# Column weights of an expert norm: folded into the expert weights, or put on the transposed rows

## The reference, cut to what matters

```python
h = h + concat(ssd_out, gmlp_out) @ w_out
h = h + hierarchical_moe(rms_norm(h, norm_ffn), ...)
h = h + sigmoid(rms_norm(h, norm_pg) @ w_pg) * rms_norm(p @ w_ple, norm_ple)

def rms_norm(x, g):
    return x * rsqrt(mean(x * x) + EPS) * g

def hierarchical_moe(t, ...):          # two experts of each row, weights comb
    for e in range(16):
        hid = silu(t @ w_gate[e]) * (t @ w_up[e])      # 1024 -> 512, twice
        y = y + comb[:, e:e + 1] * (hid @ w_down[e])   # 512 -> 1024
```

## Time and profile before

| what | value |
|---|---|
| time, median of 3 runs | 1126.4 us (1124.49 to 1126.66) |
| time of the profiled execution | 1126.14 us |
| its span on the core | 1124.2 us |
| TensorE busy | 1055.3 us (94%) |
| VectorE busy | 701.7 us (62%) |
| ScalarE busy | 504.2 us (45%) |
| POOL busy | 196.7 us (17%) |
| STT pieces of gate and up, line 1524 | 264, mean 747 ns |
| ACTIVATE pieces of gate and up, line 1920 | 264, mean 712 ns |

### The profile page before, as it was taken

One profiled execution on the slowest core, in us unless ns is written; L12 is line 12 of the kernel. 1 busy time (PEld: TensorE's weight loads), 2 busy tenths in 40 slices (PEclk: granted clock), 3 DMA queues, 4 the chain that ended last, 5 costly groups with the idle time before them and its releaser, 6 DMA issues.

```text
span 1124.2 us, 17530 instructions
## 1 busy us (share of the span) xinstructions
PE 1055.3 (94%) x6221; PEld 910.3 (81%) x6222; DVE 701.7 (62%) x1099; ACT 504.2 (45%) x872; POOL 196.7 (17%) x348
## 2 busy tenths in 40 slices
PE   7999999998999999946999999999999999999896
PEld 5777799985776788746988999898899999878685
DVE  4422575824867667256599566999946753576664
ACT  6733312033111122151588457787845652564332
POOL 3611000102233112111001000101000000065542
PEclk9999999999999999856999999999999999999998
DMA  8893400221513362157499675999966644142541
GB/s 333 269 273 73 171 1 1 76 79 56 179 61 87 109 247 85 57 179 261 140 371 372 241 278 206 384 353 384 358 237 256 239 178 168 57 168 82 166 146 56
DMA packets 71703, 209.01 MB, mean 186 GB/s; under 512 B 10863, under 2 KB 36079, under 8 KB 58730
## 3 DMA queue, kind: packets, MB, share of 16 engines
q1 hardware_dynamic: 61546, 174.02, 43.5%
q0 software_dynamic: 6512, 21.77, 5.5%
q10 hardware_dynamic: 3600, 12.62, 2.8%
HBM read 169.74 MB, written 38.65 MB: 185 GB/s over the span
## 4 chain that ended last, share of the span: by engine, by line
PE 57%; DVE 10%; issue 5%; ACT 3%; DVEq 1%; DMA 0%; POOL 0%; POOLq 0%; ACTq 0%; another core or an unknown queue 0%
PE bank L605 13%; PE bank L607 12%; PE bank L606 12%; PE bank L599 4%; DVE w_lo L1524 4%; PE bank L850 3%; PE bank L852 3%; PE bank L851 3%; PE bank L593 2%; ACT w_hi L1920 2%; PE bank L821 1%; PE bank L788 1%; DVE w_lo L1051 1%; PE bank L807 1%; PE bank L814 1%
## 5 line engine op out<-in xcount | busy, mean ns | idle before, releaser
L605 PE MATMUL bank<-w_hi,xh 128*128 128x256 f32 x768 | 220.7, 287 | 2.7 <-DVE xl L1051 2.7
L606 PE MATMUL bank<-w_lo,xh 128*128 128x256 f32 x768 | 218.4, 284 | 0.0
L607 PE MATMUL bank<-w_hi,xl 128*128 128x256 f32 x768 | 218.4, 284 | 0.0
L1524 DVE SCALAR_TENSOR_TENSOR w_lo<-raw_gu,cols,w_hi 128x512 fp32r<-128x512 f32 x264 | 178.0, 747 | 7.4 <-ACT w_hi L1920 6.3
L1920 ACT ACTIVATE w_hi<-raw_gu,cols 128x512 fp32r<-128x512 f32 x264 | 165.4, 712 | 21.1 <-PE bank L607 16.4
L605 PEld LDWEIGHTS bank<-w_hi,xh 128*128 128x128 f32 x768 | 147.9, 193 | 5.4 <-issue 3.1
L606 PEld LDWEIGHTS bank<-w_lo,xh 128*128 128x128 f32 x768 | 148.1, 193 | 0.5
L607 PEld LDWEIGHTS bank<-w_hi,xl 128*128 128x128 f32 x768 | 148.0, 193 | 0.0
L605 PE MATMUL bank<-w_hi,hid_hi 128*128 128x512 f32 x192 | 80.6, 420 | 11.6 <-DVE hid_lo L1051 11.6
L2230 POOL COPY index_u<-token_u 128x1 uint32 (+1 forms) x25 | 7.8, 311 | 428.2 <-PE bank L599 405.4
L607 PE MATMUL bank<-w_hi,hid_lo 128*128 128x512 f32 x192 | 75.3, 392 | 0.0
(11 more groups left out here) (373 smaller groups left out, 2195.6 us busy)
## 6 DMA issues: line engine op xcount, KB each, us to landing
raw_gu<-in_w_gate_up SPq DMA_DIRECT2D x64, 1024.0 KB, 4.9
raw_d<-in_w_down_rows SPq DMA_DIRECT2D x32, 1024.0 KB, 6.7
y_rows<-yb ACTq DMA_DIRECT2D x24, 512.0 KB, 6.4
raw_w<-in_w_in_blocks SPq DMA_DIRECT2D x20, 512.0 KB, 6.5
y_rows<-ones SPq DMA_DIRECT2D x16, 512.0 KB, 6.5
xr<-in_x_prompt_t SPq DMA_DIRECT2D x8, 512.0 KB, 9.2
xst<-in_x_prompt SPq DMA_DIRECT2D x8, 512.0 KB, 10.0
raw_o<-in_w_out SPq DMA_DIRECT2D x8, 512.0 KB, 3.6
```

The costliest lines, as they stand in the source:

```text
L605: nc.tensor.matmul(out, lh(k), rh(k), start=(k == 0), stop=False)
L606: nc.tensor.matmul(out, lh(k), rl(k), start=False, stop=False)
L607: last = nc.tensor.matmul(out, ll(k), rh(k), start=False, stop=(k == (K or len(ks)) - 1))
L1524: ins = V.scalar_tensor_tensor(out=gu_lo[:, k, :, cols_], in0=raw_gu[q // KC][:, k, :, :], scalar=gain(e, k), in1=gu_hi[:, k, :, cols_].bi ...
```

## The change

The expert weights are split as they are, without the columns `g`. A piece of gate and up is now two rows of 128 at once, 128x1024, a plain copy on ScalarE and a plain subtraction on VectorE, and counts two steps. The columns `g` go on the transposed rows instead: `b_xT` takes them from the banks in eight pieces of 128x128, each with its column as scale (ScalarE) or as the scalar of an STT (VectorE). Only the last of the eight counts in `xh_ready` or `xT_ready`; behind it stands a wait for the other seven. The projection of the gate stage keeps its pieces of 128x512 with columns, in functions of their own (`pg_low`, `pg_high`).

```diff
 # VectorE, split(e, at)
+                if isinstance(e, int) and e == NE:
+                    for q in steps:
+                        dve.wait_ge(s("w_high"), done + q + 1)
+                        pg_low(q // KC, q % KC)
+                elif steps[0] < 2 * KC:
+                    for q in steps[::2]:
+                        dve.wait_ge(s("w_high"), done + q + 2)
                         k, cols_ = q % KC, slice(q // KC * HE, (q // KC + 1) * HE)
-                        ins = V.scalar_tensor_tensor(out=gu_lo[:, k, :, cols_], in0=raw_gu[q // KC][:, k, :, :], scalar=gain(e, k),
-                                                     in1=gu_hi[:, k, :, cols_].bitcast(F32), op0=ALU.mult, op1=ALU.subtract)
+                        lo(gu_lo[:, k:k + 2, :, cols_], raw_gu[q // KC][:, k:k + 2, :, :], gu_hi[:, k:k + 2, :, cols_]).then_inc(s("w_split"), 2)
...
+            def pg_low(half, k):
+                cols_ = slice(half * HE, (half + 1) * HE)
+                V.scalar_tensor_tensor(out=gu_lo[:, k, :, cols_], in0=raw_gu[half][:, k, :, :], scalar=gain(NE, k),
+                                       in1=gu_hi[:, k, :, cols_].bitcast(F32), op0=ALU.mult, op1=ALU.subtract).then_inc(s("w_split"), 1)
...
             def b_xT(n):
                 dve.wait_ge(s("xh_ready"), n)
-                own.did(lo(xl[:, 0:4].rearrange("p k t -> p (k t)"), bank[0][:, :], xh[:, 0:4].rearrange("p k t -> p (k t)")))
-                lo(xl[:, 4:8].rearrange("p k t -> p (k t)"), bank[1][:, :], xh[:, 4:8].rearrange("p k t -> p (k t)")).then_inc(s("xT_ready"), 1)
+                for k in range(KC):
+                    ins = V.scalar_tensor_tensor(out=xl[:, k, :], in0=bank[k // 4][:, k % 4 * P:(k % 4 + 1) * P], scalar=gain(0, k),
+                                                 in1=xh[:, k, :].bitcast(F32), op0=ALU.mult, op1=ALU.subtract)
+                    if k + 1 < KC:
+                        own.did(ins)
+                    else:
+                        own.wait()
+                        ins.then_inc(s("xT_ready"), 1)
...
 # ScalarE, split(e, at)
+                    elif x2 and e == NE:
+                        pg_high(q // KC, q % KC)
+                    elif q % 2 == 0:
                         k, cols_ = q % KC, slice(q // KC * HE, (q // KC + 1) * HE)
-                        ins = A.activation(gu_hi[:, k, :, cols_], raw_gu[q // KC][:, k, :, :], ACT.Copy, scale=gain(e, k))
+                        A.activation(gu_hi[:, k:k + 2, :, cols_], raw_gu[q // KC][:, k:k + 2, :, :], ACT.Copy).then_inc(s("w_high"), 2)
...
             def b_xT(n):
                 act.wait_ge(s("xTp_done"), n)
-                own.did(A.activation(xh[:, 0:4].rearrange("p k t -> p (k t)"), bank[0][:, :], ACT.Copy))
-                own.wait()
-                A.activation(xh[:, 4:8].rearrange("p k t -> p (k t)"), bank[1][:, :], ACT.Copy).then_inc(s("xh_ready"), 1)
+                for k in range(KC):
+                    ins = A.activation(xh[:, k, :], bank[k // 4][:, k % 4 * P:(k % 4 + 1) * P], ACT.Copy, scale=gain(0, k))
+                    if k + 1 < KC:
+                        own.did(ins)
+                    else:
+                        own.wait()
+                        ins.then_inc(s("xh_ready"), 1)
```

More of the change, by code:

```diff
@@ L1519, in split @@
                 steps = SPLITS[at]
-                for q in steps:
-                    dve.wait_ge(s("w_high"), done + q + 1)
-                    if q < 2 * KC:
+                if isinstance(e, int) and e == NE:
[5 more added lines that the diff above has]
+                        dve.wait_ge(s("w_high"), done + q + 2)
                         k, cols_ = q % KC, slice(q // KC * HE, (q // KC + 1) * HE)
-                        ins = V.scalar_tensor_tensor(out=gu_lo[:, k, :, cols_], in0=raw_gu[q // KC][:, k, :, :], scalar=gain(e, k),
-                                                     in1=gu_hi[:, k, :, cols_].bitcast(F32), op0=ALU.mult, op1=ALU.subtract)
-                    else:
+                        lo(gu_lo[:, k:k + 2, :, cols_], raw_gu[q // KC][:, k:k + 2, :, :], gu_hi[:, k:k + 2, :, cols_]).then_inc(s("w_split"), 2)
+                else:
+                    for q in steps:
+                        dve.wait_ge(s("w_high"), done + q + 1)
                         ks = q - 2 * KC
-                        ins = lo(d_lo[:, ks, :], raw_d[:, ks, :], d_hi[:, ks, :])
-                    ins.then_inc(s("w_split"), 1)
+                        lo(d_lo[:, ks, :], raw_d[:, ks, :], d_hi[:, ks, :]).then_inc(s("w_split"), 1)
+            def pg_low(half, k):
+                cols_ = slice(half * HE, (half + 1) * HE)
+                V.scalar_tensor_tensor(out=gu_lo[:, k, :, cols_], in0=raw_gu[half][:, k, :, :], scalar=gain(NE, k),
+                                       in1=gu_hi[:, k, :, cols_].bitcast(F32), op0=ALU.mult, op1=ALU.subtract).then_inc(s("w_split"), 1)
             def final_ple(k):
@@ L1536, in final_pg @@
                 dve.wait_ge(s("w_high"), STEPS * NE + KC + PC + k + 1)
-                cols_ = slice(half * HE, (half + 1) * HE)
-                V.scalar_tensor_tensor(out=gu_lo[:, k, :, cols_], in0=raw_gu[half][:, k, :, :], scalar=gain(NE, k),
-                                       in1=gu_hi[:, k, :, cols_].bitcast(F32), op0=ALU.mult, op1=ALU.subtract).then_inc(s("w_split"), 1)
+                pg_low(half, k)
             def b_xT(n):
                 dve.wait_ge(s("xh_ready"), n)
-                own.did(lo(xl[:, 0:4].rearrange("p k t -> p (k t)"), bank[0][:, :], xh[:, 0:4].rearrange("p k t -> p (k t)")))
-                lo(xl[:, 4:8].rearrange("p k t -> p (k t)"), bank[1][:, :], xh[:, 4:8].rearrange("p k t -> p (k t)")).then_inc(s("xT_ready"), 1)
+                for k in range(KC):
[6 more added lines that the diff above has]
+                        ins.then_inc(s("xT_ready"), 1)
             def b_hidT(half, ready):
@@ L1917, in split, with pg_high @@
                         act.wait_ge(s(name), 16 * (e + earlier + 1) if x2 else act.snap(16 * e + 16 * earlier + 16))
-                    if q < 2 * KC:
-                        k, cols_ = q % KC, slice(q // KC * HE, (q // KC + 1) * HE)
-                        ins = A.activation(gu_hi[:, k, :, cols_], raw_gu[q // KC][:, k, :, :], ACT.Copy, scale=gain(e, k))
[L1921 to L1924, removed]
+                    if q >= 2 * KC:
+                        ks = q - 2 * KC
+                        A.activation(d_hi[:, ks, :], raw_d[:, ks, :], ACT.Copy).then_inc(s("w_high"), 1)
+                    elif x2 and e == NE:
+                        pg_high(q // KC, q % KC)
+                    elif q % 2 == 0:
+                        k, cols_ = q % KC, slice(q // KC * HE, (q // KC + 1) * HE)
+                        A.activation(gu_hi[:, k:k + 2, :, cols_], raw_gu[q // KC][:, k:k + 2, :, :], ACT.Copy).then_inc(s("w_high"), 2)
+            def pg_high(half, k):
+                cols_ = slice(half * HE, (half + 1) * HE)
+                A.activation(gu_hi[:, k, :, cols_], raw_gu[half][:, k, :, :], ACT.Copy, scale=gain(NE, k)).then_inc(s("w_high"), 1)
             def b_xT(n):
                 act.wait_ge(s("xTp_done"), n)
-                own.did(A.activation(xh[:, 0:4].rearrange("p k t -> p (k t)"), bank[0][:, :], ACT.Copy))
-                own.wait()
-                A.activation(xh[:, 4:8].rearrange("p k t -> p (k t)"), bank[1][:, :], ACT.Copy).then_inc(s("xh_ready"), 1)
+                for k in range(KC):
+                    ins = A.activation(xh[:, k, :], bank[k // 4][:, k % 4 * P:(k % 4 + 1) * P], ACT.Copy, scale=gain(0, k))
+                    if k + 1 < KC:
+                        own.did(ins)
+                    else:
+                        own.wait()
+                        ins.then_inc(s("xh_ready"), 1)
             def b_hidT(half, ready):
@@ L1948, in final_pg @@
                     act.wait_ge(s(f"w{2 * half + 2 * k // KC}_loaded"), 16 * (NE + 8))
-                cols_ = slice(half * HE, (half + 1) * HE)
-                A.activation(gu_hi[:, k, :, cols_], raw_gu[half][:, k, :, :], ACT.Copy, scale=gain(NE, k)).then_inc(s("w_high"), 1)
+                pg_high(half, k)
             def one_block(b, e, splits, more):
```

## The result

The changed kernel takes 1161.7 us (median of 4 runs, 1161.12 to 1162.28) against 1126.5 for the kernel before on the same chip (4 runs): ratio 1.0314, interval 1.0292 to 1.0335, slower by 35 us. The profiled execution has a span of 1160.5 us, 36.3 more than before.

A forecast was written before the change was run, and what follows sets the result against it. TensorE, busy 94%, was taken to bound the kernel, with `xh`, `xl`, `hid_lo` in series setting its expert-stage waits. 25 g - 11.7, with g = 1.88, gave +35 us on 1126.14: 1161 us, range 1138 to 1177.

The forecast's parts named there:

- The chain `xh`, `xl`, `hid_lo`: Expert stage, from the transposes' end to the down product's third quarter: 2.9 us without slack, additions move TensorE one for one.
- `xh` +1.00: ScalarE in `b_xT`: eight pieces with a column take 2.23 us against 1.23 before, +1.00 us.
- `xl` +0.88: VectorE in `b_xT`: eight pieces until the next start take 2.08 us against 1.20 before, +0.88 us.
- g = 1.88: Growth of the serial row-split work per block in `b_xT`, 1.00 + 0.88 us; bounds 0.7 to 3.2.
- Periods 20.47, 23 of them 470.8 us: Between down-product starts: short periods 18.59 + 1.88 = 20.47 us, long ones the same; all 23 together +31.6 us.
- First block +1.9: First `b_xT` stands in the open before the first matmul, where TensorE waits 2.7 us for `xl`: +1.9 us.
- The end +1.9: After the last block the gate stage waits for VectorE's projection-weight split, queued behind the last `xl`: about +1.9 us.
- the long periods: Nine down-product periods of 19.85 us: the wider split removes their 1.3 us first-quarter wait, cover 0.4 us, leaving 20.47.
- the rival of 1173 us: Nine single-block-expert periods keep their first-quarter wait and add g, +43 + 4 us; 15% together with dearer pieces.
- the dearer pieces: Row pieces in `b_xT` costing more, g = 2.5, giving 1177 us; 15% together with the long-period rival.
- 25 g - 11.7: Whole change: 25 row splits each adding g, less 11.7 us of long waits in the nine periods: +35 us.
- The clock: Rival: TensorE's clock drops to 1.2 GHz after each block's wait, some +4.5 us x 23, about 1265 us; 3%.

The follow-up runs named there:

- e3: Changed kernel, but VectorE starts `xl` on the first four pieces while ScalarE makes the other four: 1134.5 us, ratio 1.0063.
- e6: Changed kernel with sixteen pieces of 128x64 in place of eight of 128x128 in `xh` and `xl`: 1253.9 us (one run).
- e8: Kernel before with the rows taken from the banks in eight plain 128x128 pieces, no column operand: 1133.8 us (one run).
- e2: Kernel before, narrow weight split kept, rows taken in eight pieces with a column of ones: 1159.2 us (one run), again 1160.7 us, ratio 1.0309.
- e1: Kernel before with the wide weight split alone, rows in two pieces as before, norm columns left out: 1116.2 us, ratio 0.9922.
- e9: Changed kernel with `xh` counted by halves and VectorE doing six `xl` pieces, second-half `hid_lo`, two `xl` pieces: 1123.9 us, ratio 0.9994.
- e11: Changed kernel, `xh` counted by halves, five `xl` pieces before second-half `hid_lo`, three behind, TensorE waiting later for each half's last two weight steps: 1119.6 us, ratio 0.9951.
- e7: Kernel before with the wide split, rows in two plain pieces, POOL multiplying the gathered rows by the norm columns before the transposes: 1146.5 us, ratio 1.0170.

## Why the prediction was right, and where its working was not

The time was 1161 forecast, 1161.7 measured. By its own steps:

- **The chain `xh`, `xl`, `hid_lo` sets TensorE one for one.** Shown: e3 takes four pitches out of it and every period falls by 1.0 us; e6 adds 2.23 us to it and the wait grows by as much.
- **`xh` +1.00.** Eight take 2.17 to 2.18 us where 2.23 was worked out, +0.95. A piece is 382 ns, not 364, and the pitch 0.255, not 0.267. The piece was put together from a plain copy and the price of a column. e8 has both alone: a plain piece 308 ns (277 was taken) and so 74 for the column (87 was taken); the errors have opposite signs. The pitch, which counts seven times, is 0.166 for a plain piece (0.18 was taken) and 0.089 more with the column (0.087 was taken). By the figures of the Trainium skill, ScalarE: Activation LUTs, section What ACT_TABLE_LOAD costs, the estimate was 2.44; the measurement decides for 2.17.
- **`xl` +0.88.** 659.54 to 661.62 is 2.08 us, as forecast; a piece is 343 ns (339 forecast).
- **g = 1.88.** 20.39 - 18.59 = 1.80 us, 0.08 under the forecast, 0.05 of it in `xh`.
- **Periods 20.47, 23 of them 470.8 us.** 471.0 measured, of which 1.6 are the clock (below). So the agreement to 0.2 us is luck in part: 23 periods of 20.39 make 469.0, 1.8 under the forecast.
- **First block +1.9.** 534.65 - 532.71 = 1.94; TensorE's wait for `xl` goes from 2.7 to 4.5 us. Here too some is luck: with the same wait of 4.5 us the first period of e2 is 20.16 us, 1.2 over the 18.98 of before, where after has 20.98. The stage begins at the clock's lower level, and from 520 to 526 us the granted clock is 0.71 in e2, 0.73 before and 0.55 in after.
- **The end +1.9.** From the last down product's start to the end of the span it is 154.8 us against 152.2, +2.6. The split that was named (`wple_lo`) starts 7.25 us behind that start (1012.91) against 5.70 before (977.67), which is 1.55 of them. But TensorE's wait for it didn't grow (2.0 us against 2.2): the last down product is late itself, with a wait of 1.49 us for `hid_lo` at its third quarter (1010.40). The other 1.1 us is open.

The three pieces make 31.7 + 1.9 + 2.6 = 36.2 us of the span's 36.3.

**The step that failed** is the account of the long periods: "hid_lo of the first half comes just in time", thanks to the wider split, with "thin cover, 0.4 us", and the rival of 1173 us where the cover fails. (By the sum's own terms, 16.1 and 15.6, the cover is 0.5.) e2 has no wider split, TensorE waits 1.0 to 1.4 us for its first `hid_lo` in the nine blocks, and its stage is 489.5 us, that of after within 2.2 (1.6 of them the clock). A late first quarter costs nothing as long as it eats into the wait at the third, so the real cover was the forecast one plus most of the 1.8 us wait that the change itself makes. The rival had no place to happen; I had given it 15% of the chance with the dearer pieces. The cover that was forecast did fail in the kernel after: in two of the nine blocks `hid_lo` ends 0.1 us behind the transposes, and two first-quarter waits of 0.25 us are left (718.74 in the fence above). Their periods are 20.40 and 20.41 us, so they cost nothing.

It follows that the wide split is worth 10 us alone (e1) and next to nothing beside the pieces (after against e2, 1.0314 and 1.0309). Its gain isn't cancelled by a loss elsewhere: the limit that it lifts was no longer the one that held. The 11.7 in the sum "25 g - 11.7" was right as a number and wrong as a saving of the split: it is what the long waits of before cover of g.

**The clock**, held at 3%, happened once. Windows of the kernel after, and that block in its timeline of PE:

```profile
718.00:738.00 20.00, 18.45 (x131) 16.81 (x130) 17.88 (x26) 15.48 (x25) 1.14 (x2) 1.00 0.95 360
744.00:748.00 4.00, 4.00 (x12) 3.08 (x12) 4.00 (x4) 3.05 (x4) 0.00 (x0) 0.59 0.71 239
...
536.00:743.00 207.00, 188.70 (x1330) 173.30 (x1328) 142.23 (x224) 125.68 (x224) 12.27 (x21) 1.00 0.70 265
748.00:985.00 237.00, 217.80 (x1561) 201.93 (x1559) 151.59 (x238) 130.34 (x235) 12.58 (x22) 1.00 0.68 256
```

```profile
743.68 0.65 PE L605 MATMUL bank<-w_hi,hid_hi 128*128 128x512 f32 x1 [1.81 <-DVE hid_lo L1051]
744.12 0.63 PE L606 MATMUL bank<-w_lo,hid_hi 128*128 128x512 f32 x1
744.55 0.63 PE L607 MATMUL bank<-w_hi,hid_lo 128*128 128x512 f32 x1
```

Behind a wait of 1.81 us the matmuls start 0.43 us apart instead of 0.23 until 747.1, eight of them, at the lower of the two levels, 1.2 GHz; the clock of the four microseconds is 0.59. The block takes 21.99 us, 1.6 more. The same wait of 1.81 us at 662.09 left the clock at 1.00, and so did those of all other blocks from 536 to 985 us; in the two runs of e2, with 14 waits of 1.79 to 1.81 us each, it is 1.00 from 536 to 1003 us. The rival's price of 4.5 us a block, from a quarter of the matmuls at the lower level, was too high: 1.6 in after and in most blocks of e6. In every block it came only in e6, behind waits of 4.0 us. Why one of sixteen equal waits did it in after is open.

## What to carry to other kernels

Find the chain that ends a period and count its length from the event that starts it; work added there costs itself in every period, whatever the totals say: 14 us less work on two engines came with 35 us more time. Two limits of one period don't add, so price each edit alone and both together (here -10, +34 and +35). Where many small pieces must stand in such a chain, hand over after half of them and put the consumer that TensorE waits for between them: that took 38 us off the changed kernel (e9), and 42 with a later wait for the weights and one piece fewer ahead (e11).

## What the runs showed of the hardware

- A column operand costs 74 ns on a 128x128 ACTIVATE out of a bank (382 against 308) and 63 on a subtraction (343 for the STT against 280), about a quarter of a plain small piece, and the pitch rises with it: 0.255 and 0.26 us against 0.17 and 0.20 for plain ones (e8: (1.47 - 0.308) / 7 and (1.67 - 0.280) / 7).
- Half the columns save far less than half the time: 128x64 takes 364 ns against 382 on ScalarE, 275 against 343 on VectorE (e6, means by shape).
- A subtraction of 128x1024 on VectorE took up to 3.44 us instead of 1.22 beside POOL's multiplication of the same size, which took 2.33 to 3.45 (e7). VectorE's copies of 128x512 out of a bank took 0.68 to 0.69 us, beside it or not.
- The clock fell behind one of sixteen waits of 1.8 us (after) and behind waits of 4.0 us throughout (e6); the block then took 1.6 us longer, in e6 in most blocks.
